# The memory rows' norm dealt over seven chunks of an FFN, and the two attentions of the first mixer exchanged

## The reference, cut to what matters

```python
def first_block(x, mem, ...):
    for layer in range(2):
        g = ln_gains[layer]
        x = x + 0.5 * swiglu(rms_norm(x, g[0]), ffn1_w_in[layer], ffn1_w_out[layer])
        h = rms_norm(x, g[1])
        x = x + (even_mixer if layer % 2 == 0 else odd_mixer)(h, ...)
        x = x + memory_cross_attention(rms_norm(x, g[2]), rms_norm(mem, g[3]), ...)
        x = x + 0.5 * swiglu(rms_norm(x, g[4]), ffn2_w_in[layer], ffn2_w_out[layer])

def even_mixer(h, w_in, ...):
    a_q, a_k, a_v, a_f, b_q, b_k, b_v = split_cols(h @ w_in, EVEN_SIZES)
    aq, ak = rms_norm(a_q, qk_gains[0]), rms_norm(a_k, qk_gains[1])   # 8 heads of 64
    logf = jax.nn.log_sigmoid(a_f + f_bias)
    a_out = forgetting_attention(aq, ak, a_v, cumsum(logf))           # causal, bias from the gates
    bq, bk = rope(rms_norm(b_q, qk_gains[2])), rope(rms_norm(b_k, qk_gains[3]))
    b_out = differential_attention(bq, bk, b_v, lam)                  # softmax 1 - lam * softmax 2
    b_out = rms_norm(b_out, subln_gain) * (1.0 - lambda_init)
    return jnp.concatenate([a_out, b_out], axis=-1) @ w_out

def memory_cross_attention(h, mem_n, w_q, w_kv, ...):
    k, v = split_cols(mem_n @ w_kv, (1024, 1024))
    ...
```

## Time and profile before

| | |
|---|---|
| median of 3 runs | 2210.24 us (2206.32 to 2214.51) |
| profiled execution | 2217.5 us |
| its span | 2215.6 us |
| TensorE busy | 2165.2 us |
| VectorE busy | 1507.8 us |
| ACT busy | 1180.9 us |
| first FFN | about 10 to 205 us of the span |
| first mixer up to the output projection | about 210 to 392 us |
| third FFN's memory norm | about 676 to 700 us |
| second mixer | to about 985 us |

### The profile page before, as it was taken

The page is one execution under the profiler, slowest core; times in us unless marked ns, Lnnn a source line. Parts: engine busy times, 40 slices in busy tenths (PEclk is TensorE's granted clock), DMA queues, the critical chain, the costliest instruction groups (busy, mean ns, idle before and its releaser), DMA issues.

```text
span 2215.6 us, 44906 instructions
## 1 busy us (share of the span) xinstructions
PE 2165.2 (98%) x18339; PEld 2120.5 (96%) x18339; DVE 1507.8 (68%) x2247; ACT 1180.9 (53%) x1851; POOL 111.6 (5%) x133
## 2 busy tenths in 40 slices
PE   7999998999999999999999999999999999999998
PEld 7999888899999999989999999989999999999998
DVE  7756678676667667676766666688766666667664
ACT  6645546564456444465654554546554544546543
POOL 2000000010001000010000000101000000001001
PEclk9999999999999999999999999999999999999999
DMA  9555533275555556443655665634665655536553
GB/s 289 173 179 177 155 119 114 88 248 190 190 193 189 180 182 223 143 143 108 213 194 186 196 192 193 228 127 151 199 195 186 202 191 189 183 105 200 191 184 103
DMA packets 384635, 392.77 MB, mean 177 GB/s; under 512 B 6848, under 2 KB 383040, under 8 KB 384304
## 3 DMA queue, kind: packets, MB, share of 16 engines
q1 hardware_dynamic: 382400, 382.84, 53.4%
q0 software_dynamic: 1600, 6.78, 0.8%
q10 hardware_dynamic: 432, 0.26, 0.1%
HBM read 388.81 MB, written 1.05 MB: 176 GB/s over the span
## 4 chain that ended last, share of the span: by engine, by line
PE 87%; DVE 6%; ACT 4%; issue 2%; POOL 1%; DMA 0%; SPq 0%; POOLq 0%; DVEq 0%; ACTq 0%
PE acc L614 25%; PE acc L618 24%; PE acc L615 24%; DVE w_lo L1432 2%; PE acc L632 2%; PE acc L634 2%; PE acc L633 2%; ACT w_hi L1009 2%; PE acc L583 1%; PE acc L585 1%; PE acc L584 1%; POOL t L1951 1%; PE wide L809 0%; PE wide L707 0%; PE wide L691 0%
## 5 line engine op out<-in xcount | busy, mean ns | idle before, releaser
L1432 DVE TENSOR_TENSOR w_lo<-raw,w_hi 128x1024 fp32r<-128x1024 f32 (+2 forms) x790 | 899.0, 1141 | 482.2 <-ACT w_hi L1009 480.0
L1009 ACT ACTIVATE w_hi<-raw 128x1024 fp32r<-128x1024 f32 (+2 forms) x790 | 775.9, 988 | 823.3 <-PE acc L618 751.0
L614 PE MATMUL acc<-hn_hi,w_hi 128*128 128x256 f32 x3328 | 789.0, 279 | 14.2 <-ACT w_hi L1009 14.2
L615 PE MATMUL acc<-hn_lo,w_hi 128*128 128x256 f32 x3328 | 783.5, 278 | 0.0
L614 PEld LDWEIGHTS acc<-hn_hi,w_hi 128*128 128x128 f32 x3328 | 627.3, 188 | 18.1 <-issue 15.5
L615 PEld LDWEIGHTS acc<-hn_lo,w_hi 128*128 128x128 f32 x3328 | 627.2, 188 | 0.6 <-issue 0.5
L618 PE MATMUL acc<-hn_hi,w_lo 128*128 128x256 f32 x3328 | 449.3, 278 | 0.0
L618 PEld LDWEIGHTS acc<-hn_hi,w_lo 128*128 128x128 f32 x3328 | 412.2, 188 | 0.0
L614 PE MATMUL acc<-hid_hi,w_hi 128*128 128x256 f32 x1408 | 331.6, 277 | 0.0
L615 PE MATMUL acc<-hid_lo,w_hi 128*128 128x256 f32 x1408 | 331.6, 277 | 0.0
L614 PEld LDWEIGHTS acc<-hid_hi,w_hi 128*128 128x128 f32 x1408 | 264.9, 188 | 0.0
(11 more groups left out here) (252 smaller groups left out, 2201.0 us busy)
## 6 DMA issues: line engine op xcount, KB each, us to landing
raw<-in_ffn_w_in SPq DMA_DIRECT2D x87, 1024.0 KB, 5.1
raw<-in_ffn_w_out SPq DMA_DIRECT2D x32, 1024.0 KB, 5.2
raw<-in_ffn_pre_w_gate SPq DMA_DIRECT2D x22, 1024.0 KB, 5.2
raw<-in_ffn_pre_w_up SPq DMA_DIRECT2D x22, 1024.0 KB, 5.2
raw<-in_ffn_post_w_gate SPq DMA_DIRECT2D x22, 1024.0 KB, 5.3
raw<-in_ffn_post_w_up SPq DMA_DIRECT2D x22, 1024.0 KB, 5.2
raw<-in_x_w_kv SPq DMA_DIRECT2D x16, 1024.0 KB, 5.4
raw<-in_ffn_pre_w_down SPq DMA_DIRECT2D x16, 1024.0 KB, 5.1
```

Of the source, the lines that this page charges most:

```text
L614: nc.tensor.matmul(bank, wh[:, j, :], a_hi[:, u.k0 + j, :], start=u.first and j == 0, stop=False)
L615: nc.tensor.matmul(bank, wh[:, j, :], a_lo[:, u.k0 + j, :], start=False, stop=False)
L1009: nc.scalar.activation(w_hi[:, u.slot, 0:u.nk, :], raw[:, u.raw % RING, 0:u.nk, P * u.half:P * u.half + P], ACT.Copy).then_inc(w_hi_ready, 1)
L1432: nc.vector.tensor_tensor(w_lo[:, u.slot, 0:u.nk, :], raw[:, u.raw % RING, 0:u.nk, P * u.half:P * u.half + P], w_hi[:, u.slot, 0:u.nk, :]. ...
```

## The change

In both FFNs with a memory norm the eight squares are done in two fours, behind chunks 1 and 2; TensorE's sum stands behind the unit with index 14 and is followed by three transposes of `x`; ACT's root stands behind chunk 4; VectorE scales two blocks behind each of the chunks 5 to 8, ACT writes two high parts behind each of 6 to 9, VectorE two low parts behind each of 7 to 10.

In the first mixer the order becomes `af`, `bq`, `bk`, `gate_biases`; the norm of B's heads with `bv` and two `memk0` units; the rotation with two; attention B with `aq` and `ak`; the norm of B's output with two units of `av`; the norm of A's heads with the other two and four `memk0b` units; attention A with the lists of D. B's output takes blocks 0 to 3 of `cat` and A's blocks 4 to 7, so the two halves of the output projection's weights change places (`turn`). The squares of the cross attention's keys move from B to A, and three buffers get other places.

```diff
--- before.py
+++ after.py
+MEM_SQUARED, MEM_SUMMED = 1, 4
@@ plan_stream
             add("af", [(w, 1536)], KB, "F", "hn", gen, width=P)
+            project(w, ("bq", 1544, 512), ("bk", 2056, 512), ("bv", 2568, 512))
+            add("memk0", cols(kv, 0, D // 2), KB, "F", "mn", fill)
             project(w, ("aq", 0, 512), ("ak", 512, 512), ("av", 1024, 512))
-            add("memk0", cols(kv, 0, D // 2), KB, "F", "mn", fill)
-            project(w, ("bq", 1544, 512), ("bk", 2056, 512), ("bv", 2568, 512))
             add("memk0b", cols(kv, D // 2, D // 2), KB, "F", "mn", fill)
...
-        add(f"mixout{n}a", cols(wo, 0, D), KB // 2, "F", "mn", fill)
-        add(f"mixout{n}", cols(wo, 0, D), KB, "F", "mn", fill, row0=KB // 2)
+        turn = 0 if n else KB // 2
+        add(f"mixout{n}a", cols(wo, 0, D), KB // 2, "F", "mn", fill, turn=turn)
+        add(f"mixout{n}", cols(wo, 0, D), KB, "F", "mn", fill, row0=KB // 2, turn=turn)
@@ order, first mixer
-                    project("aq")
+                    project("bq")
                     s.forget_sums(c)
-                    project("ak")
+                    project("bk")
                     s.gate_biases(c)
-                    project("av")
-                    head(work[:, 16:24, :], 8, 64, ["even"] * 4 + [("even", 1)] * 4, memk[0:1], memk[1:4])
-                    bv, late, memv, half = span("bv"), span("memk0b"), span("memv0"), span("mixout0a")
-                    att("A", deal(span("bq", "bk") + bv[0:2], 1, 0, 1, 1, 1, 1, 1, 1, 1, 0, 2, 0))
-                    head(work[:, 24:32, :], 8, 64, [("even", 2)] * 4 + [("even", 3)] * 4, bv[2:4], late[0:3])
-                    rotate(work[:, 24:32, :], perm_rope, rope_c, rope_s, late[3:4] + memv[0:2])
-                    att("B", [[memv[2:4], []], [memv[4:6], []], [memv[6:8] + [(0, 4)], []], [half[0:1], half[1:2]], [half[2:3], []], [half[3:4], []]])
-                    head(cat[:, 4:8, :], 4, 128, ["subln"] * 4, half[4:6], half[6:8])
-                    split_cat(4, 8)
+                    bv, av, late, memv, half = span("bv"), span("av"), span("memk0b"), span("memv0"), span("mixout0a")
+                    head(work[:, 24:32, :], 8, 64, [("even", 2)] * 4 + [("even", 3)] * 4, bv[0:2], bv[2:4] + memk[0:2])
+                    rotate(work[:, 24:32, :], perm_rope, rope_c, rope_s, memk[2:4])
+                    att("B", deal(span("aq", "ak"), 2, 0, 2, 0, 1, 0, 1, 0, 1, 0, 1, 0))
+                    head(cat[:, 0:4, :], 4, 128, ["subln"] * 4, av[0:1], av[1:2])
+                    head(work[:, 16:24, :], 8, 64, ["even"] * 4 + [("even", 1)] * 4, av[2:4], late)
+                    att("A", [[memv[0:2], []], [memv[2:4], memv[4:6]], [memv[6:8] + [(0, 4)], []], [half[0:1], half[1:3]], [half[3:4], half[4:5]],
+                              [half[5:6], half[6:8]]], final=True)
@@ TensorE, ffn_up
-                    if n is not None and j == 11:
+                    if n is not None and j == 4 * MEM_SUMMED - 2:
                         pe.wait_ge(squares_added, 7 * (c.norm + 1))
                         nc.tensor.matmul(wide[:, 1, 0:T], ones, t1[:, 0, :], start=True, stop=True).then_inc(sums_done, 1)
+                        for b in range(3):
+                            nc.tensor.transpose(wide[:, 0, P * b:P * b + P], x[:, b, 0:P], ident)
@@ ACT, ffn_up
-                    if n is not None and ch == 1:
+                    if n is not None and MEM_SQUARED <= ch < MEM_SQUARED + 2:
                         act.wait_ge(mem_in, 16 * (n + 1))
-                        for k in range(8):
+                        for k in range(4 * (ch - MEM_SQUARED), 4 * (ch - MEM_SQUARED) + 4):
                             nc.scalar.activation(t1[:, k, :], keep[:, k, :], ACT.Square).then_inc(squares, 1)
-                    if n is not None and ch == 3:
+                    if n is not None and ch == MEM_SUMMED:
                         act.wait_ge(sums_done, c.norm + 1)
                         rsqrt(t2[:, 0, :], 1.0 / D, wide[:, 1, 0:T], t2[:, 1, :]).then_inc(std_done, 1)
...
-                        for k in range(8):
+                    if n is not None and MEM_SUMMED + 2 <= ch < MEM_SUMMED + 6:
+                        for k in range(2 * (ch - MEM_SUMMED) - 4, 2 * (ch - MEM_SUMMED) - 2):
                             act.wait_ge(normed, 8 * n + k + 1)
                             nc.scalar.activation(mn_hi[:, k, :], t1[:, k, :], ACT.Copy).then_inc(mn_hi_ready, 1)
@@ VectorE, ffn_up
-                    if n is not None and ch == 3:
+                    if n is not None and MEM_SUMMED + 1 <= ch < MEM_SUMMED + 5:
                         dve.wait_ge(std_done, c.norm + 1)
...
+                        for k in range(2 * (ch - MEM_SUMMED) - 2, 2 * (ch - MEM_SUMMED)):
+                            nc.vector.scalar_tensor_tensor(t1[:, k, :], keep[:, k, :], gains[:, gain + k:gain + k + 1],
+                                                           t2[:, 0, :], ALU.mult, ALU.mult).then_inc(normed, 1)
+                    if n is not None and MEM_SUMMED + 3 <= ch < MEM_SUMMED + 7:
+                        for k in range(2 * (ch - MEM_SUMMED) - 6, 2 * (ch - MEM_SUMMED) - 4):
...
@@ attend, ACT (and the same for key_adds on VectorE)
-                    if m == 4 and kind in "BD":
-                        key_squares("BD".index(kind))
+                    if m == 4 and kind in "AD":
+                        key_squares("AD".index(kind))
@@ buffers
-        key_sq = [work[:, 24:32, :], work[:, 8:16, :]]
-        key_sum, key_rstd = work[:, 32:36, :], work[:, 36:40, :]
+        key_sq = work[:, 8:16, :]
+        key_sums_at, key_rstds = [work[:, 36:40, :], work[:, 32:36, :]], [work[:, 32:36, :], work[:, 36:40, :]]
```

More of the change, by code:

```diff
@@ L354, in attention @@
         def attention(kind):
-            q0, k0, bias, v, out0 = {"A": (16, 20, gate_pair, vals(32, 4), 0), "B": (24, 28, lambda m: both(chunked), vals(36, 4), 4),
+            q0, k0, bias, v, out0 = {"A": (16, 20, gate_pair, vals(32, 4), 4), "B": (24, 28, lambda m: both(chunked), vals(36, 4), 0),
                                      "D": (16, 20, band_pair, vals(36, 4), 4), "E": (28, 32, lambda m: both(dil_bias), vals(40, 4), 0)}[kind]
@@ L765, in key_sums @@
                     for b in range(2):
-                        mm = nc.tensor.matmul(wide[:, 2 + b, :], ones, key_sum[:, 2 * b:2 * b + 2, :].rearrange("p b t -> p (b t)"),
+                        mm = nc.tensor.matmul(wide[:, 2 + b, :], ones, key_sums_at[n][:, 2 * b:2 * b + 2, :].rearrange("p b t -> p (b t)"),
                                               start=True, stop=True)
@@ L1200, in key_squares @@
                 act.wait_ge(biased, 16 if n == 0 else 28)
-                nc.scalar.activation(key_sq[n], memk_out, ACT.Square).then_inc(keys_sq, 1)
+                nc.scalar.activation(key_sq, memk_out, ACT.Square).then_inc(keys_sq, 1)
             def cross_attend(c, n, xq, xo):
@@ L1211, in key_stats @@
                     act.wait_ge(keys_sums, n + 1)
-                    o = key_rstd.rearrange("p (b a) t -> p b (a t)", a=2)
+                    o = key_rstds[n].rearrange("p (b a) t -> p b (a t)", a=2)
                     rsqrt(o, 1.0 / CW, wide[:, 2:4, :], o).then_inc(keys_std, 1)
@@ L1601, in mem_low @@
                                 .then_inc(mn_lo_ready, 1)
-                        for k in range(9):
-                            if k < 8:
-                                nc.vector.scalar_tensor_tensor(t1[:, k, :], keep[:, k, :], gains[:, gain + k:gain + k + 1],
-                                                               t2[:, 0, :], ALU.mult, ALU.mult).then_inc(normed, 1)
-                            if k:
-                                mem_low(k - 1)
             def head_norm(c, src, nb, per, gain, before, after):
@@ L1686, in attend @@
                         normalise(m - 1)
-                    if m == 5 and kind in "BD":
-                        key_adds("BD".index(kind))
+                    if m == 5 and kind in "AD":
+                        key_adds("AD".index(kind))
                     take(between[m][0])
@@ L1695, in key_adds @@
                 dve.wait_ge(keys_sq, n + 1)
-                pairs = key_sq[n].rearrange("p (h e) t -> p h e t", e=2)
-                nc.vector.tensor_tensor(key_sum, pairs[:, :, 0, :], pairs[:, :, 1, :], ALU.add).then_inc(keys_added, 1)
+                pairs = key_sq.rearrange("p (h e) t -> p h e t", e=2)
+                nc.vector.tensor_tensor(key_sums_at[n], pairs[:, :, 0, :], pairs[:, :, 1, :], ALU.add).then_inc(keys_added, 1)
             def cross_keys(c, n):
@@ L1718, in bias @@
                         ins = nc.vector.scalar_tensor_tensor(prob[:, g % 3, qt, :], wide[:, h % 2, T * qt:T * qt + T],
-                                                             query_rstd[:, h, qt:qt + 1], key_rstd[:, h, :], ALU.mult, ALU.mult)
+                                                             query_rstd[:, h, qt:qt + 1], key_rstds[n][:, h, :], ALU.mult, ALU.mult)
```

1 line of the change is left out of this document (removed), and 2 rows, old and new, of the table dest.

## The result

The changed kernel has a median of 2191.41 us (4 runs, 2189.56 to 2192.83), the kernel before, with one more run, 2211.61 us (4 runs, 2206.32 to 2214.51). The ratio is 0.9911, with a 95% interval of 0.9889 to 0.9932: 20.2 us, or 0.9%, faster, where 7.2 us were forecast. The prediction was wrong.

The account below looks back on a forecast made before the run. TensorE, busy 98%, was taken as the bound, with only waits and below-full-clock stretches recoverable: mixer 12.0 - 2.2 - 4.2 = 5.6, FFNs 1.6, together 7.2 us off the 2210.24 median, 2203.0 us; range 2197 to 2209.

Parts of the forecast that it names:

- FFNs, 1.6 us: Two FFNs with a memory norm: 2.1 us of waits go, less 0.5 for transposes; 1.6 us gained, 1.1 to 2.1.
- Triples, 0.5: Three new transposes behind each FFN's norm sum: 0.25 us each FFN, 0.5 in both; per-FFN bounds 0 to 0.5.
- Mixer, 12.0 reachable: First mixer, plus a second-mixer dip: 3.7 + 6.6 us of waits and 1.7 of clock loss within the change's reach.
- B's start, 2.2: Attention B, now first: less cover for head norm and rotation, late turns and scores cost 2.2 us, bounds 1.0 to 4.5.
- A's end like D's, 4.2: Attention A, now last: waits of 1.7 and 0.8 us and a 1.7 clock dip, as in D; bounds 2.5 to 5.5.
- rival 2: Late part of the mixer runs free: no clock dip, D's 2.5 us shrink; 2198.8 to 2201.3 us, chance 0.17.
- mixer 5.6: First mixer's net gain: 12.0 us reachable less 2.2 at B's start and 4.2 at A's end, 5.6 us.
- Carried over to the median unscaled: Profiled execution before was 7.3 us above the runs' median, 2210.24; this distance was kept, turning 2210.3 into 2203.0 us.
- The tail under 2199.2: Unknown costs all low (1.0 in B, 2.5 in A, 2.1 in the FFNs) give 2198.1 us; chance 0.12.
- rival 5: VectorE's queue, B's sums to A's third pair: low-part weight waits laid open, 14.4 us; slower, 2217.4 us, chance 0.04.
- rival 3: Sub-norm's wait only moves, to in front of A's head norm: 3.8 us comes back, 2206.8 us, chance 0.08.
- Rival 6: ACT's table switch before B's Ln costs more than its load, a 1.2 us drain: 2204.2 us, chance 0.02.

Follow-up runs that it names:

- norm part: The kernel before with only the change's memory-norm edits in both FFNs (dealt over seven chunks, sum behind unit 14, transposes): 2200.32 us, ratio 0.9973.

## Why the prediction was wrong, point by point

- **"An edit that takes no matmul away can therefore give back only what TensorE now waits, or runs below full clock."** This is the step that failed. 21.7 of 26.9 us came out of busy time, 17 of them at a granted clock of 1.00. The views that I had read held the sign: the page gives's matmuls in groups of one shape, one kind of operand and unequal means (279, 278, 277 ns and more, where the fast pace records 276), and the prediction itself says "units of 2.83 us, as the projections run at elsewhere" beside units of 2.72 in the earlier trace rows. I took the 0.11 us for noise around one price. It was a loss of 4% on 636 us. What the runs showed in its place: equal matmuls have two prices at full clock, 113.4 and 117.8 ns, and a wait in front of a projection can leave it at the dearer one to its end. Two waits of 0.5 us put in cost 7.6 us, eight cost 28.9.
- **FFNs, 1.6 us.** The mechanism was right: all waits of the earlier trace rows went, with the cover that was counted, and the dealing hid all its pieces. The term was mis-sized, since a wait was priced at its own length. Measured with the rest held still, the norm part gives 8.3 us in the median and 6.8 in the mean: 2.1 us of waits and some 5 to 6 behind them, nearly all of it pace, which the two FFNs lose on average when a wait lets it be drawn.
- **Triples, 0.5.** The lower bound, zero, was right: the kernel without them runs as fast.
- **Mixer, 12.0 reachable.** Right for the waits: the 3.8 and the 0.7 us of the earlier trace rows went, as did the 1.3 us one for the Square and the 1.7 us one for the first maximum of the earlier trace rows.
- **B's start, 2.2.** 2.1 us were measured, but not where the count had them. The scores of pair 1 wait for nothing (0.2 counted), the turns wait 1.5 (2.9 and less counted), and 0.6 is the sub-norm's sum, which was not in the count at all.
- **A's end like D's, 4.2.** Of its waits, 1.7 came as 1.7, 0.8 as 1.2, and a weighing adds 0.4: 3.3 against 2.5. D itself now waits 1.2 and 0.4 too, so the nearest row was right in kind, and varies by some tenths. The dip of 1.7 us was not there, as rival 2 has it. Of the eight profiles with A in last place two have it (the second one of the kernel after, at 347 us, and the one with eight waits), so on average it costs some 0.4 us, and taking it whole was too much.
- **Taken together, mixer 5.6.** 9.1 measured on top of the norm part. Waits give 4.9 (10.3 less 5.4), and the dips the rest, as far as profiles of one execution each can say: the one behind the 3.8 us wait cost 3.4 us and not 1.7 in the norm part alone, and the one in the second mixer, in code that was not touched, is in the profiles of before and of the norm part alone and not in that of after. 4.9 + 3.4 + 1.7 = 10.0, which is enough for the 9.1. (That last one stands in all five profiles with B at the first mixer's end and in two of the eight with A there; what links the two, no run shows.)
- **Carried over to the median unscaled.** The profiled execution of before was an unlucky draw, 7.3 us above its median, slow through most of both memory FFNs. That 7 us is not a fixed distance: the same two kernels give 26.9 us by profiles and 20.2 by medians. Part of the distance to the forecast is then luck of the draws: with before in its lowest group, as in a third of its runs, the change would have measured some 12.6 us.
- **The tail under 2199.2.** The case in "Chances and range" is added up wrongly: 1.0 in B and 2.5 in A leave 8.5 of the mixer's 12.0, with 2.1 in the FFNs 10.6 us, which is 2199.6 and not 2198.1. By its own costs even the best case of the forecast did not reach 2199.2, so its chance of 0.12 there had nothing behind it. The 2221.2 of rival 5 with rival 3 likewise lies just inside 2221.3, not over it.
- **The rivals.** 1 (VectorE is the bound in B) and 5 (slower) did not come; 3 (the sub-norm's wait only moved) came as 0.6 us of 3.8; 4 (the dealing fails) not at all. Rival 6, and the rule beside it: in front of B's norm ACT has

```profile
235.06 1.28 ACT L1037 ACT_TABLE_LOAD   x1
236.41 1.97 ACT L1041 ACTIVATE t<-wide,colc 128x2048 f32<-128x2048 f32 x1
```

Ln starts 0.07 us behind the load's end. The Trainium skill's drain ("ScalarE: Activation LUTs", What ACT_TABLE_LOAD costs) of about 1.4 us does not show here either.

What no rival held was a change of pace. Rival 2 came nearest, and its end of 2198.8 is still 7.4 us off. The range missed since all its cases shared the same first sentence.

## What to carry to other kernels

Before pricing a change to a kernel whose TensorE is always busy, divide busy time by count in windows of one kind of work, and compare the mean lengths of equal matmuls: 4% between stretches at the same granted clock is time that an edit can give back. A short wait in front of a long projection is then worth not its length but its length plus what the work behind it may lose, here 3 us on average for 0.5; and in this study every kernel with such waits in front of a long projection had runs 9 to 18 us apart, unless a sum and triple followed, and those without 2 to 4, so a wide spread is a sign to look for. Where runs fall into groups, compare means and lowest runs as well as medians. A dummy sum and triple brought the fast pace back, at 0.8 us a piece in the traces, but the kernels with them stayed 4.8 us above the one without the waits, or no better than before, so taking the wait away is the better cure.

## What the runs showed of the hardware

- **Two paces at full clock.** Pairs of weight load and 256-column matmul go at 113.4 or 117.8 ns, recorded as 276 or 281 ns, at a granted clock of 1.00 in both. The matmul starts 110 ns behind its weight load in the one and 114 to 115 in the other. The Trainium skill, "TensorE: Matmul & The Clock Gate", Back-to-back issue gap, gives N / 2.4 + 2.5 ns for an isolated matmul, so 109 ns at this width, and for pairs of weight load and matmul one spacing each at widths of 128 (81 ns) and 512 (131 ns). It has none for pairs at 256 and mentions no second pace; the traces decide.
- **It holds across hundreds of matmuls, and turns at breaks.** The "69 times of 70" of the expectation above does not come out of the traces; what does is sharper. In all thirteen profiles an fp32 sum with a triple directly in front of a projection, and no idle moment, was followed by the fast pace 120 times of 120, 31 of them out of the slow one. Where the cross attention's four sums of keys stand between triple and projection, the pace stayed what it had been, 15 times fast and 11 times slow. So it did behind a bare fp32 sum without idling, 15 times of 15, as in the kernel after without its triple. With an idle moment in front, sum and triple ended slow both times. A plain idle moment was followed by either pace. Other fp32 groups turn it: behind a weighing inside the cross attention it was slow 22 times of 24 (six profiles). Why, and what differs inside the engine, no run here tells, nor whether it is the idling itself or what it does to the order of things behind it.
- **Half-rate stretches come and go.** Those of 3.4 us, or 6.8, stand behind waits of 1.7 to 4 us in some executions and not in others; the one behind the 3.8 us wait was in each of the four profiles with it. One comes with no wait at all, at `gate_biases` (220 to 230 us above), and was missing in two profiles of thirteen.
